# Second mixer in eight steps: attention of one pair of heads beside the next pair's three strips, forget gates in free rows of the keys

## What is computed

```python
N_SB_HEADS = 8; N_FOX_HEADS = 8; HEAD_DIM = 64; BLOCK_Q = 128; SEQ = 512; D_MODEL = 1024

def stick_breaking_attention(q, k, v):          # per block of 128 queries
    z = einsum('bhqd,bhkd->bhqk', q, k) * scale
    mask = arange(end)[None, :] < arange(start, end)[:, None]
    log_beta = log_sigmoid(z)
    log_keep = where(mask, log_sigmoid(-z), 0.0)
    later = cumsum(log_keep, axis=3, reverse=True) - log_keep
    w = where(mask, exp(log_beta + later), 0.0)
    return einsum('bhqk,bhkd->bhqd', w, v)

def forgetting_attention(q, k, v, log_f_cum):   # per block of 128 queries
    z = einsum('bhqd,bhkd->bhqk', q, k) * scale
    z = z + log_f_cum[:, :, start:end, None] - log_f_cum[:, :, None, :end]
    mask = arange(end)[None, :] <= arange(start, end)[:, None]
    return einsum('bhqk,bhkd->bhqd', softmax(where(mask, z, -inf)), v)

def hybrid_mixer(h, w_in, b_f, g_q, g_k, w_o):
    sb_q, sb_k, sb_v, fox_q, fox_k, fox_v, fox_f = split(h @ w_in)   # 6 x 512 and 8 columns
    sb_out = stick_breaking_attention(sb_q, sb_k, sb_v)
    fq, fk = rms_norm(fox_q, g_q), rms_norm(fox_k, g_k)              # per head
    log_f_cum = cumsum(log_sigmoid(fox_f + b_f), axis=1)
    fox_out = forgetting_attention(fq, fk, fox_v, log_f_cum)
    return concatenate([sb_out, fox_out]) @ w_o
```

## Time and profile before

| | us |
|---|---|
| median of 3 runs | 1961.7 |
| lowest and highest | 1960.43 and 1966.07 |
| profiled execution | 1959.5 |
| its span, from the first to the last instruction | 1957.7 |
| PE busy in it | 1901.6 (97%) |
| DVE, ACT, POOL busy | 991.8, 688.4, 45.9 |
| mean granted TensorE clock | 0.987 |

### The profile page before, as it was taken

How to read it: one execution, slowest core, us unless ns; L and a number is a source line. 1 busy time by engine, 2 the same in 40 slices (tenths; PEclk the granted TensorE clock), 3 DMA queues, 4 the chain that set the end, 5 groups by cost and what they waited for, 6 DMA issues and landing times.

```text
span 1957.7 us, 21498 instructions
## 1 busy us (share of the span) xinstructions
PE 1901.6 (97%) x8929; PEld 1583.3 (81%) x8929; DVE 991.8 (51%) x1335; ACT 688.4 (35%) x1027; POOL 45.9 (2%) x75
## 2 busy tenths in 40 slices
PE   6999999999999999999999999999999999999998
PEld 5688888887888888888888888777778878888887
DVE  5555553457766757753333336246576553333332
ACT  5444442334323323442222224245644442222222
POOL 0000000000000000000000001000021000000001
PEclk9999999999999999889999999999999999999999
DMA  3222222364675665423333332321100123333333
GB/s 120 65 84 86 76 83 86 97 181 135 186 223 176 207 182 179 137 73 98 97 96 98 96 87 78 98 58 40 43 23 1 46 84 97 97 97 97 97 91 92
DMA packets 321718, 200.07 MB, mean 102 GB/s; under 512 B 6696, under 2 KB 311126, under 8 KB 321622
## 3 DMA queue, kind: packets, MB, share of 16 engines
q1 hardware_dynamic: 320128, 196.17, 34.4%
q0 software_dynamic: 640, 2.10, 0.3%
q10 hardware_dynamic: 854, 0.43, 0.1%
HBM read 196.57 MB, written 2.10 MB: 101 GB/s over the span
## 4 chain that ended last, share of the span: by engine, by line
PE 85%; DVE 6%; ACT 4%; DMA 2%; issue 2%; POOL 0%; SPq 0%; DVEq 0%; ACTq 0%
PE ps L1140 84%; DMA w_raw<-in_w_ffn_up 2%; PE ps L1143 1%; ACT w_hi L346 1%; DVE p_lo L1028 1%; DMA w_raw<-in_w_ffn_down 1%; DVE mod_acc L767 0%; DMA x_in<-in_x 0%; DVE t_b L738 0%; DVE att_a L1018 0%; DVE p_hi L1027 0%; ACT att_b L643 0%; DVE t_b L943 0%; ACT y_hi L531 0%; DVE p_lo L863 0%
## 5 line engine op out<-in xcount | busy, mean ns | idle before, releaser
L1140 PE MATMUL ps<-u_hi,w_hi 128*128 128x512 f32 x1688 | 666.5, 395 | 7.7 <-DVE u_lo L726 3.3
L1140 PE MATMUL ps<-u_lo,w_hi 128*128 128x512 f32 x1688 | 660.4, 391 | 0.0
L1140 PE MATMUL ps<-u_hi,w_lo 128*128 128x512 f32 x1688 | 660.3, 391 | 0.0
L705 DVE TENSOR_TENSOR w_lo<-w_raw,w_hi 128x1024 fp32r<-128x1024 f32 (+2 forms) x307 | 365.2, 1190 | 310.0 <-ACT w_hi L346 308.8
L346 ACT ACTIVATE w_hi<-w_raw 128x1024 fp32r<-128x1024 f32 (+2 forms) x307 | 314.4, 1025 | 243.9 <-DMA w_raw<-in_w_down 77.6
L1140 PEld LDWEIGHTS ps<-u_hi,w_hi 128*128 128x128 f32 x1688 | 319.3, 189 | 79.0 <-issue 10.4
L1140 PEld LDWEIGHTS ps<-u_hi,w_lo 128*128 128x128 f32 x1688 | 318.9, 189 | 67.0
L1140 PEld LDWEIGHTS ps<-u_lo,w_hi 128*128 128x128 f32 x1688 | 319.3, 189 | 66.0 <-issue 1.5
L1140 PE MATMUL ps<-y_hi,w_hi 128*128 128x512 f32 x656 | 255.9, 390 | 1.2 <-DVE y_lo L945 1.2
L1140 PE MATMUL ps<-y_hi,w_lo 128*128 128x512 f32 x656 | 255.3, 389 | 0.0
L1140 PE MATMUL ps<-y_lo,w_hi 128*128 128x512 f32 x656 | 255.2, 389 | 0.0
(11 more groups left out here) (257 smaller groups left out, 1484.2 us busy)
## 6 DMA issues: line engine op xcount, KB each, us to landing
mod_raw<-in_w_mod SPq DMA_DIRECT2D x72, 512.0 KB, 4.5
w_raw<-in_w_in SPq DMA_DIRECT2D x71, 512.0 KB, 3.8
w_raw<-in_w_ffn_up SPq DMA_DIRECT2D x44, 512.0 KB, 5.0
w_raw<-in_w_gate SPq DMA_DIRECT2D x44, 512.0 KB, 3.8
w_raw<-in_w_up SPq DMA_DIRECT2D x44, 512.0 KB, 3.8
w_raw<-in_w_down SPq DMA_DIRECT2D x32, 512.0 KB, 3.8
w_raw<-in_w_ffn_down SPq DMA_DIRECT2D x16, 512.0 KB, 5.9
w_raw<-in_w_down SPq DMA_DIRECT2D x16, 384.0 KB, 3.3
```

The costliest lines, as they stand in the source:

```text
L705: e.tensor_tensor(w_lo[u % SLOTS][:, 0:n_k, :], w_raw[u % SLOTS][:, 0:n_k, :], f32(w_hi[u % SLOTS][:, 0:n_k, :]), ALU.subtract).then_inc(l ...
L1140: return e.matmul(out_, lhsT, rhs, start=start, stop=stop, skip_group_check=skip)
```

## The change

The second mixer's units become one list `proj` and its work eight steps, one for each pair of heads: in step i PE computes the attention of pair i and multiplies the three strips of pair i+1, on all engines in that order. Steps 0 to 3 are stick-breaking, 4 to 7 softmax.

- q, k and v of a stick-breaking pair are cut straight from the PSUM bank of their unit; `sq`, `sk`, `sv`, `fv` go. q and k of a softmax pair go to `fq` and `fk`, one tile each, are normalised and cut in the step before their attention.
- `p_hi`, `p_lo` have a tile for each head. The PSUM banks of the two heads swap each step (`slot_banks`). In `sb_cut` each subtraction stands behind the next cast.
- The gates: eight rows of the negated running sum are written once by POOL into the rows of `k_hi[:, h]`, `k_lo[:, h]` that belong to the other head and were zero, and a row of ones into `q_hi` there for each pair. The products with `f_hi` and `f_lo` go. k has a tile for each head.
- All `keep_busy` calls of the mixer go, 28 + 4 * (40 + 12) + 16.
- The first three units of `w_o` are opened in the last step with seven of their eight parts and closed when the last pair is ready (`open_strip`, `head_product`); the third uses PSUM bank 3. The heads go to `heads`, and from there to `u_hi`, `u_lo` late in step 6; `y_hi`, `y_lo` of the other stages lie at the same place.
- The first block's attention uses tiles of its own names, `w_p_hi` and `w_p_lo`; the output tiles are `out_sb`.

The core of the diff (the helpers are the old ones with new indices):

```diff
-SB_BANKS = ((2, 3, 4), (5, 6, 7))
-FOX_BANKS = ((2, 3, 4), (5, 6, 1))
+ATT_BANKS = ((2, 3, 4), (5, 6, 7))
+HEAD_ORDER = (0, 1, 2, 3, 6, 4, 5, 7)
+OPEN_STRIPS = 3
+def slot_banks(i, n):
+    return ATT_BANKS[(i + n) % 2]
...
 def scalar(e):
+            for i in range(N_SB):
+                u = p0 + 3 * (i + 1)
+                sb_soft_plus(i, 0)
+                sb_soft_plus(i, 1)
+                cut_hi(u + 2)
...
+                    stage_q(ubank(u), 0)
...
+                cut_hi(u + 3)
...
+                    stage_k_both(ubank(u + 1))
+                sb_weights(i, 0)
...
+                cut_hi(u + 4)
+                sb_weights(i, 1)
+                if i + 1 == N_SB:
+                    roots(i, 0)
+                take_v(i + 1)
+                if i + 1 == N_SB:
+                    stage_normed(0)
+                e.wait_ge(at_valued, 2 * i + 2)
+                e.activation(heads[:, i, :], bank(slot_banks(i, 0)[0]), ACT.Copy).then_inc(at_out, 1)
+                stage_v(i + 1)
+            for i in range(N_SB, N_STEPS):
+                u = p0 + 3 * (i + 1)
+                t = i + 1 - N_SB
...
+                fox_exp(i, 0)
+                fox_exp(i, 1)
+                cut_hi(u + 2)
...
+                    take_q(i + 1)
+                fox_cut(i, 0)
...
+                square_q(t)
+                cut_hi(u + 3)
+                square_k(t)
+                fox_cut(i, 1)
+                roots(i, t)
+                cut_hi(u + 4)
+                stage_normed(t)
+                take_v(i + 1)
...
 def gpsimd(e):
+            e.wait_ge(sb_masked, 6 * N_SB)
+            for h, rows in ((0, slice(HEAD_DIM, HEAD_DIM + N_FOX)), (1, slice(0, N_FOX))):
...
+                e.tensor_copy(k_hi[rows, h, :], nf[rows, :]).then_inc(aux_set, 1)
+                e.wait_ge(aux_set, 2 * h + 1)
+                e.tensor_tensor(k_lo[rows, h, :], nf[rows, :], f32(k_hi[rows, h, :]), ALU.subtract).then_inc(aux_set, 1)
+            for t in range(N_STEPS - N_SB):
+                e.wait_ge(at_scored, 2 * (N_SB + t))
+                for h, rows in ((0, slice(HEAD_DIM, HEAD_DIM + N_FOX)), (1, slice(0, N_FOX))):
+                    c = C_IDENT + (rows.start + 2 * t + h)
+                    e.wait_ge(aux_set, 4 + 2 * t + h)
+                    e.tensor_copy(q_hi[rows, h, :], consts[rows, c:c + 1].broadcast_to([N_FOX, SEQ])).then_inc(aux_set, 1)
 def tensor(e):
-                    mm(reg, ones_r[:, :], f_hi[:, n, 0:w], False, False)
-                    mm(reg, ones_r[:, :], f_lo[:, n, 0:w], False, False)
...
+            def open_strip(c):
+                u = U["w_o"] + c
+                e.wait_ge(lo_cut, u + 1)
+                if c < 2:
+                    e.wait_ge(bank_read[u % 2], u // 2)
+                for pos in range(KC - 1):
+                    e.wait_ge(u_lo_set, FILL["heads"] * KC + pos + 1)
+                    head_product(u, pos)
...
+            unit_pair(u, u_act, (u_lo_set, FILL["mix2"] * KC))
+            unit(p0 + 1, u_act)
...
+            unit(p0 + 2, u_act)
...
+            for i in range(N_STEPS):
+                u = p0 + 3 * (i + 1)
+                last = i + 1 == N_STEPS
...
+                (sb_scores if i < N_SB else fox_scores)(i, 0)
+                if i == 0:
+                    e.wait_ge(nf_set, 1)
+                elif last:
+                    e.wait_ge(u_lo_set, FILL["heads"] * KC + 5)
+                else:
+                    e.wait_ge(at_out, i)
+                (sb_scores if i < N_SB else fox_scores)(i, 1)
+                if last:
+                    open_strip(0)
+                    fox_turn(i, 0)
+                    open_strip(1)
+                    fox_turn(i, 1)
+                    tri_values(i, 0)
+                    tri_values(i, 1)
+                    open_strip(2)
+                    break
+                unit(u, u_act)
+                if i < N_SB:
+                    unit(u + 1, u_act)
+                    sb_suffix(i, 0)
+                    sb_suffix(i, 1)
+                else:
+                    fox_turn(i, 0)
+                    unit(u + 1, u_act)
+                    fox_turn(i, 1)
+                if i + 1 >= N_SB:
+                    head_totals(i, i + 1 - N_SB)
+                unit(u + 2, u_act)
+                tri_values(i, 0)
+                tri_values(i, 1)
+                project_v(i + 1)
+            e.wait_ge(u_lo_set, (FILL["heads"] + 1) * KC)
+            for c in range(OPEN_STRIPS):
+                head_product(U["w_o"] + c, KC - 1).then_inc(unit_done, 1)
+            for c in range(OPEN_STRIPS, KC):
                 unit(U["w_o"] + c, u_act)
-            keep_busy(28, 4)
-                keep_busy(40, 0)
-                keep_busy(12, 0)
-            keep_busy(16, 0)
-            unit_pair(U["w_o"], u_act, (u_lo_set, FILL["heads"] * KC))
```

More of the change, by code:

```diff
@@ L196, in two_blocks @@
         with ExitStack() as r2:
[L197 to L201, removed]
+            p_hi = [sb(f"p_hi{n}", [P, TRI], F32R, r2) for n in range(2)]
+            p_lo = [sb(f"p_lo{n}", [P, TRI], F32R, r2) for n in range(2)]
+        with ExitStack() as r2:
+            out_sb = sb("out_sb", [P, KC, SEQ], F32, r2)
         with ExitStack() as r2:
@@ L1054, in fox_peak, with sb_cut @@
-            def fox_peak(m, pair):
-                n = m % 2
+            def sb_cut(n, ready, n0):
+                first = own[0]
+                for k in range(4):
+                    if k < 3:
+                        _, at, w = PACKED[k]
+                        e.wait_ge(ready, n0 + k + 1)
+                        e.tensor_copy(p_hi[n][:, at:at + w], att[n][:, at:at + w]).then_inc(dve_own, 1)
+                        own[0] += 1
+                    if k:
+                        _, at, w = PACKED[k - 1]
+                        e.wait_ge(dve_own, first + k)
+                        e.tensor_tensor(p_lo[n][:, at:at + w], att[n][:, at:at + w], f32(p_hi[n][:, at:at + w]), ALU.subtract).then_inc(p_cut, 1)
@@ L1092, in vector, with fox_cut @@
[L1092 to L1095 removed]
+            def fox_cut(i, n):
+                for k, (b, at, w) in enumerate(packed(slot_banks(i, n))):
+                    e.wait_ge(pt_hi, 6 * (i - N_SB) + 3 * n + k + 1)
+                    e.tensor_tensor(p_lo[n][:, at:at + w], ps[:, b, 0:w], f32(p_hi[n][:, at:at + w]), ALU.subtract).then_inc(p_cut, 1)
@@ L1243, in win_scores @@
                     bs = slice(b * P, (b + 1) * P)
-                    ins = three(own, (q_hi[:, h, bs], q_lo[:, h, bs]), (k_hi[:, ks], k_lo[:, ks]), False, True)
+                    ins = three(own, (q_hi[:, h, bs], q_lo[:, h, bs]), (k_hi[:, 0, ks], k_lo[:, 0, ks]), False, True)
                 ins.then_inc(w_scored, 1)
@@ L1325, in tensor, with project_v, sb_scores @@
             mod_columns(3)
+            p0 = U["proj"]
             u = U["gate_f"]
+            NF = TB * N_FOX
+            fl = gate[:, 2 * NF:3 * NF]
+            def project_v(i):
+                e.wait_ge(proj_v, i + 1)
+                for tb in range(TB):
+                    ins = turn(ps[:, (p0 + 3 * i + 2) % 2, tb * P:(tb + 1) * P], v_t[:, tb * P:(tb + 1) * P])
+                ins.then_inc(pv_turned, 1)
+            def sb_scores(i, n):
+                for j in range(TB):
+                    js = slice(j * P, (j + 1) * P)
+                    ins = three(tri(slot_banks(i, n), j), (k_hi[:, 0, js], k_lo[:, 0, js]), (q_hi[:, n, j * P:SEQ], q_lo[:, n, j * P:SEQ]),
+                                j < 3, True, skip=j == 3)
+                ins.then_inc(at_scored, 1)
```

646 lines of the change are left out of this document (333 added, 313 removed).

## The result

The changed kernel takes **1927.0 us** (median of 4 runs, 1925.6 to 1927.6) against 1961.6 us before (1960.4 to 1966.1): ratio 0.9818, 95% interval 0.9801 to 0.9835. It is 34.6 us faster. I had forecast 1895 and a range of 1884 to 1911, so the direction was right and the time was 32 us off, outside the range.

A forecast was written before the change was run, and what follows sets the result against it. TensorE bounds the mixer. Mixer parts 28.0 + 92.2 + 33.4 + 90.3 + 57.9 = 301.8, plus restarts 1.6 and clock 2.5, against 371.9: 66.0 us saved, forecast 1895 us, range 1884 to 1911.

The forecast's parts named there:

- One strip of 24 products: 5.46: PE price in us of one weight strip at warm clock, start to start, read from w_o's rows before the change.
- Opening: Mixer's first stretch, 83.0 us before: nine strips, three v turnings and some waits leave it; 28.0 us taken.
- Stick-breaking steps: Steps 0 to 2: scores, three strips, suffixes, values and v at 30.7 us each, with no waits on p_lo.
- Step 3: Last stick-breaking step: 30.7 us plus head totals and a 0.9 us wait for q and k cuts, 33.4 in all.
- Softmax steps: Steps 4 to 6: 29.3 us of PE work plus waits of 0.5 (keys) and 0.3 (divisions), 30.1 us each.
- Last step and w_o: Final softmax attention with three open w_o strips, their closing, and five more strips, waits included: 57.9 us.
- The new wait: At w_o's fourth strip: its weight cut stands behind the first strip's residual, only 1.4 us hide it; 2.3 us of wait.
- Clock: Allowance of 2.5 us for clock falls, from narrow matmuls at the opening's end and the new wait in w_o.
- A: Softmax steps run at their own chain's pace: 2 to 4 us more in steps 3 to 6, 1903 to 1911; chance 0.18.
- B: Clock falls at step boundaries, behind narrow products with short stops: one fall a step, +13.6 us, 1906; chance 0.12.
- C: Slower than before: mixer's clock stays down while PE is busy, strips cost twice; 2100 if wholly at 0.50; chance 0.02.
- D: Steps don't overlap because a bank or staged tile frees late: 2.6 us wait a pair, +21, 1916; chance 0.05.

The follow-up runs named there:

- the run with the tile put back: Changed kernel plus an unused tile of 128 bytes a partition where f_col stood, no instruction changed: 1889.9 us, ratio 0.9628 to the kernel before.
- the run with delays: Kernel with the 128-byte tile plus two VectorE delays, ahead of one softmax step's divisions and the next's key low parts: first absorbed, second lengthens its step by 0.60 us.
- the run with the early cut: Kernel with the 128-byte tile, w_o's fourth strip's two cuts made before the last head's values are taken: 1888.0 us, wait 1.4 us.
- twelve kernels above: The kernel before, the same with f_col moved, the changed kernel, and nine versions of it with unused bytes ahead of u_hi, w_hi or x: 1889.2 to 1995.5 us.

## Why the prediction missed, point by point

**The step that failed** is the price "One strip of 24 products: 5.46" and the sum made from it: only the mixer's time was subtracted from the profiled execution, so the 7128 strip matmuls, 6336 of them outside the mixer, were taken to cost after the change what they cost before. They cost 2.5% more (a strip some 5.6 us), 37.2 us in all by the run with the tile put back. The diff did show the line `f_col` going and the tile named `align` beside it; I priced instructions and waits, and no term or rival was about where tiles stand. With the distance restored the time is 1889.9, inside the range and 5 us under the forecast.

**The mixer**, by the sum's own steps against the run with the tile (its pitch is that of the prices). From start to start on PE: 1210.97, first scores 1238.46, then 1270.80, 1301.70, 1332.60, 1365.89, 1395.34, 1424.79, 1454.24, end 1513.21.

- Opening: forecast 28.0, measured 27.5, of which some 1.7 is a fall of the clock; without it 25.8. Over by 2.2. The stop for `nf_lo` is gone; the rest I have not traced.
- Stick-breaking steps: forecast 30.7 and 0.2 for restarts, measured 30.90, without waits. Step 0 took 32.34 with a fall of the clock in it (the row below). Step 3: 33.4 forecast, 33.29 measured; its wait on `k_lo` was 0.48, not 0.9.
- Softmax steps: 30.1 forecast, 29.45 measured. The two waits (0.5 and 0.3) didn't come, as the run with delays bears out: at the keys the chain is level with PE, at the divisions well ahead of it.
- Last step and w_o: 57.9 forecast, 58.97 measured. The new wait came where I had put it and was 3.1 us, not 2.3. The chain was the right one, as the run with the early cut shows, but I ended it one instruction too early, at the `w_lo` cut: the second residual behind it (0.74, of which 0.65 after the cut's end) and the handoff (0.15, from its end at 1507.96 to PE's start at 1508.11) are what is missing.
- Clock: 2.5 allowed; two falls of 3.4 us cost some 3.3 in all, one in the opening and one in step 0, none in the steps without fillers after that. (In the changed kernel itself it fell once more, to 0.53 for 3.6 us behind the 3.1 us wait of w_o.)

```profile
1238.20:1241.70 3.50, 3.50 (x15) 3.21 (x14) 0.76 (x2) 1.20 (x3) 0.00 (x0) 0.51 0.13 39
```

Together 302.2 for 305.9. In the changed kernel as it stands 306.8, since 33 strips cost 0.13 us more each, 4.4 of the 4.6 between the two. That it matches my number is luck: the mixer without the slower strips is 3.7 us shorter than I summed up.

**The rivals.** A: no; steps have no wait of 2 us, and a delay ahead of the divisions costs nothing. B: no; the granted clock is 1.00 in both kinds of step. The short stops that it supposed between groups of matmuls weren't there: PE is busy for 31.32 of 31.32 and 29.67 of 29.67 us. So these runs don't tell what such stops would do to the clock. C: no sign; in the old stretch that it was built on, the strip matmuls at clock 0.50 follow each other at 427 ns (837.68 to 842.38 us), 1.9 times 226.7 and not twice. D: no wait for a bank inside a step. None of the five cases held what happened, and the time of 1927 lies between them, above the forecast, A, B and D and below C; giving the forecast and the rivals 0.97 for faster was right only because the mixer's gain was larger than the loss.

## What to carry to other kernels

When a change adds, removes or resizes a tile, work out where the tiles behind it go: here a tile of 128 bytes was worth 37 us (1889.9 against 1927.0), half of the 72 us that the restructured mixer gives with the tile in place. For streams of such matmuls (fp32r, 512 columns, a weight load ahead of each) keep the distance between moving and stationary tiles a multiple of 256 bytes (226.7 ns a matmul here, 232.3 to 233.2 at the other distances run), and count matmuls in a stretch of unchanged code before and after; busy shares hide a slower pitch (PE 497.65 of 500 us busy at 226.7 ns, 498.92 at 232.3). The kernel before without 208 of its fillers took 1964.1 us, so they cost it nothing; what they stood for was a place where strips could go. So look for the stage whose independent work can stand there.

## What the runs showed of the hardware

The pitch of a 512-column matmul at full clock is 226.7 ns or 232.3 to 233.2, and the distance modulo 256 bytes between its moving and stationary operands picks which (twelve kernels above, each as the rule says, all with fp32r operands and 128 x 128 weights). Offsets of 32, 128 and 192 cost about the same (233.2, 232.3 to 232.9 and 233.2 ns); others weren't run; weight loads stay at 188 ns in all twelve. I had not expected any dependence on a tile's place.
